# A two-part transformer kernel: row statistics of eight norms kept 128x512 instead of 128x4

## The reference

```python
def _layer_norm(x, eps):
    mu = jnp.mean(x, axis=-1, keepdims=True)
    xc = x - mu
    return xc * lax.rsqrt(jnp.mean(xc * xc, axis=-1, keepdims=True) + eps)

def _rmsnorm(x, w):
    return x * lax.rsqrt(jnp.mean(x * x, -1, keepdims=True) + NORM_EPS) * w
```

## Time and profile before

| | us |
|---|---|
| median of 3 runs | 3008.81 |
| lowest, highest | 3007.4, 3012.82 |
| the profiled execution, its own time | 3008.55 |
| its span in the profile | 3006.8 |

### The profile page before, as it was taken

One profiled execution on the slowest core, in us unless ns is written; L12 is line 12 of the kernel. 1 busy time (PEld: TensorE's weight loads), 2 busy tenths in 40 slices (PEclk: granted clock), 3 DMA queues, 4 the chain that ended last, 5 costly groups with the idle time before them and its releaser, 6 DMA issues.

```text
span 3006.8 us, 38616 instructions
## 1 busy us (share of the span) xinstructions
PE 2838.2 (94%) x16220; PEld 2225.1 (74%) x16220; DVE 1456.4 (48%) x2103; ACT 1023.1 (34%) x1526; POOL 1.4 (0%) x6
## 2 busy tenths in 40 slices
PE   5999999998999999979999999999999879899998
PEld 1476577657888877768788887888877568688886
DVE  1148444754533456454454345533455676454344
ACT  0035434543322335412432223322234432332222
POOL 0000000000000000000000000000000000000000
PEclk9999989997999999899899999999999899899998
DMA  9221112111323222100122323223232100122322
GB/s 387 85 70 64 49 56 77 64 49 50 108 85 110 79 85 96 41 32 29 64 92 88 109 80 96 98 83 110 78 95 77 57 22 4 57 91 84 109 81 70
DMA packets 65116, 245.02 MB, mean 81 GB/s; under 512 B 7216, under 2 KB 7344, under 8 KB 63536
## 3 DMA queue, kind: packets, MB, share of 16 engines
q1 hardware_dynamic: 64656, 238.36, 23.5%
q0 software_dynamic: 288, 4.19, 0.4%
HBM read 240.43 MB, written 2.10 MB: 81 GB/s over the span
## 4 chain that ended last, share of the span: by engine, by line
PE 91%; DVE 4%; ACT 3%; issue 1%; DMA 1%; SPq 0%; ACTq 0%; DVEq 0%
PE bank L367 89%; ACT work L1392 1%; DVE work L1961 1%; PE bank L550 1%; DMA work<-w_ada 1%; ACT weights_high L1426 1%; DVE residual L1961 1%; DVE weights_low L1975 0%; ACT normed L1392 0%; ACT silu_gate L1392 0%; ACT L1392 0%; PE bank L1150 0%; DVE work L2348 0%; DVE work L2650 0%; DVE silu_gate L2664 0%
## 5 line engine op out<-in xcount | busy, mean ns | idle before, releaser
L367 PE MATMUL bank<-normed,weights_high 128*128 128x512 f32 x4848 | 1544.1, 400 | 25.6 <-ACT normed L1392 22.0
L367 PEld LDWEIGHTS bank<-normed,weights_high 128*128 128x128 f32 x4848 | 914.8, 191 | 252.3 <-issue 62.3
L367 PE MATMUL bank<-normed,weights_low 128*128 128x512 f32 x2424 | 957.4, 395 | 0.0
L1975 DVE TENSOR_TENSOR weights_low<-ring,weights_high 128x1024 fp32r<-128x1024 f32 (+2 forms) x431 | 483.9, 1126 | 526.1 <-ACT weights_high L1426 522.8
L1426 ACT ACTIVATE weights_high<-ring 128x1024 fp32r<-128x1024 f32 (+2 forms) x431 | 420.7, 979 | 931.4 <-PE bank L367 931.3
L367 PEld LDWEIGHTS bank<-normed,weights_low 128*128 128x128 f32 x2424 | 463.4, 191 | 98.8
L367 PE MATMUL bank<-hidden,weights_high 128*128 128x512 f32 x1408 | 433.4, 389 | 0.0
L367 PEld LDWEIGHTS bank<-hidden,weights_high 128*128 128x128 f32 x1408 | 264.3, 188 | 54.8
L2190 DVE TENSOR_TENSOR silu_gate<-bank,rstd 128x512 f32<-128x512 f32 x176 | 120.9, 691 | 340.8 <-PE bank L367 336.0
L367 PE MATMUL bank<-hidden,weights_low 128*128 128x512 f32 x704 | 273.9, 389 | 0.0
L367 PE MATMUL bank<-work 64*64 64x64 f32 (+7 forms) x1632 | 161.2, 320 | 4.2 <-DVE work L2650 3.2
(11 more groups left out here) (222 smaller groups left out, 1897.7 us busy)
## 6 DMA issues: line engine op xcount, KB each, us to landing
ring<-w_k SPq DMA_DIRECT2D x303, 512.0 KB, 3.2
work<-w_ada SPq DMA_DIRECT2D x6, 4096.0 KB, 20.9
ring<-w_d SPq DMA_DIRECT2D x64, 384.0 KB, 3.0
ring<-w_d SPq DMA_DIRECT2D x64, 320.0 KB, 2.9
work<-dft_in POOLq DMA_DIRECT2D x2, 2048.0 KB, 8.1
constants<-cst_in SPq DMA_DIRECT2D x1, 2304.0 KB, 8.0
residual<-x_in SPq DMA_DIRECT2D x1, 2048.0 KB, 13.3
out_dram<-residual SPq DMA_DIRECT2D x8, 256.0 KB, 2.0
```

The source lines that it names most:

```text
L367: return pe.matmul(o, lhsT, rhs, start=start, stop=stop, skip_group_check=True)
L1975: ve.tensor_tensor(WL[:, u % SPLIT, 0:w], RING[:, u % SLOTS, 0:w], WH[:, u % SPLIT, 0:w].bitcast(F32), ALU.subtract).then_inc(unit_split, 1)
```

## The change

The layer norms and the feed-forward pre-norms no longer go through 128x4. Their mean square is made as the mean is, with `onesD` as the stationary tile and the 128x512 squares as the moving one: eight products in a layer norm, one on the summed squares in a feed-forward. The result is 128x512, the same in every partition. ScalarE's root and VectorE's reciprocal run over 128x512, the reciprocal straight into `RSTD[:, 1, :]`, which VectorE's products read. The spreading products of these eight norms, the wait for them, and the copy to `RSTD[:, 1, :]` in the feed-forwards go. Mixer pre-norms and post-norms stay as they are (`compact`).

```diff
+        def compact(norm):
+            return norm[0] == "post" or norm[0] == "pre" and norm[1].startswith("mix")
...
             def layer_norm(norm, after):
                 mean_over_features(norm, "mean", lambda k: X[:, k, :], PS[6], after)
-                rms_of(norm, *[(tile(k), act_done("sq", norm, k)) for k in range(KT)])
-                spread(norm)
+                mean_over_features(norm, "ms", lambda k: tile(k), PS[7], lambda k: act_done("sq", norm, k))
...
                         unit_product(u0 + j, ffn_bank("pair", q, j // 2, j % 2)[:], lambda x: H[:, x, :],
-                                     lambda x: H[:, KT + x, :], 0, KT, KT, ("pre", f) if q == 0 and j == LEAD + 1 else None)
+                                     lambda x: H[:, KT + x, :], 0, KT, KT)
                         if q == 0 and j == LEAD:
-                            rms_of(("pre", f), (tile(0), dve_done("sum", f)))
+                            pe.wait_ge(*dve_done("sum", f))
+                            step(mm(PS[7][:], cst("onesD"), tile(0)), "ms", ("pre", f))
...
             def root(norm):
                 act.wait_ge(*pe_done("ms", norm))
-                a(RSTD[:, 0, 0:4], PS[7][:, 0:4], ACT.Sqrt, "sd", norm,
+                w = TT if compact(norm) else T
+                a(RSTD[:, 0, 0:w], PS[7][:, 0:w], ACT.Sqrt, "sd", norm,
...
                         root(("pre", f))
-                        kept_rstd(("pre", f))
...
             def reciprocal_std(norm):
                 dve.wait_ge(*act_done("sd", norm))
-                d(ve.reciprocal(RSTD[:, 0, 4:8], RSTD[:, 0, 0:4]), "rstd", norm, chain=False)
+                if compact(norm):
+                    d(ve.reciprocal(RSTD[:, 0, 4:8], RSTD[:, 0, 0:4]), "rstd", norm, chain=False)
+                else:
+                    d(ve.reciprocal(RSTD[:, 1, :], RSTD[:, 0, :]))
...
                 reciprocal_std(norm)
-                dve.wait_ge(*pe_done("spread", norm))
                 for k in range(KT + 1):
                     if k < KT and first:
-                        d(stt(tile(8 + k), tile(8 + k), MOD[:, l, 8 + k:9 + k], PS[7][:], ALU.mult, ALU.mult),
+                        d(stt(tile(8 + k), tile(8 + k), MOD[:, l, 8 + k:9 + k], RSTD[:, 1, :], ALU.mult, ALU.mult),
                           "t", f"first{l}", k, chain=False)
                     elif k < KT:
-                        d(stt(X[:, k, :], tile(8 + k), v("lng", 8 * l + k), PS[7][:], ALU.mult, ALU.mult),
+                        d(stt(X[:, k, :], tile(8 + k), v("lng", 8 * l + k), RSTD[:, 1, :], ALU.mult, ALU.mult),
                           "xn", norm, k, chain=False)
...
                 low(lows_first + LEAD + SPLIT)
-                dve.wait_ge(*act_done("rstd", ("pre", name)))
+                if compact(("pre", name)):
+                    dve.wait_ge(*act_done("rstd", ("pre", name)))
```

## The result

| | before | after |
|---|---|---|
| median, us | 3009.66 | 2986.49 |
| lowest, highest | 3007.4, 3012.82 | 2984.06, 2987.57 |
| the profiled execution, its own time | 3008.55 | 2984.06 |
| its span | 3006.8 | 2982.3 |

The ratio is 0.9921, 95% interval 0.9906 to 0.9936: faster by some 23 us, where 17 had been forecast. The direction came out as forecast, and so did what each of the eight places costs after the change; some 5 us of the gain were in no step of the sum.

What follows compares the result with a forecast made beforehand. TensorE was taken to bound the kernel, busy 94% of the span. Layer norms 13.2 plus feed-forward pre-norms 3.9 gave 17.1 us, so 2991.7 us against the median, with 2986 to 2999 for 8 in 10.

Steps and rivals of the forecast that it cites:

- the sum: Whole kernel: layer norms 13.2 plus feed-forward pre-norms 3.9 give 17.1 us saved, other moved work costed at nothing.
- What bounds the kernel: TensorE, busy 94% of the span: norm latency counts in the layer norms, only TensorE time in the dense feed-forward stream.
- The layer norms, 13.2 us: Four layer norms: chains shorter by 4.45, 2.54, 1.71 and 4.46 us, together 13.2 us.
- The new path: Each layer norm, first square product to VectorE's next product: 1.28 + 14 x 0.429 + 0.80 + 3.38 = 11.47 us.
- Full clock in the wide products: Layer norms: all 16 wide instructions of a mean square run at full clock, 0.429 us apart.
- the first rival: Layer norms: the 1.4 us silence lowers the clock, wide instructions at half clock, 27.4 us more, 3019.1 us; chance 0.05.
- the partly slow one: Layer norms: a quarter of the 64 wide instructions at half rate gives back 6.9 us, 2998.6 us; chance 0.12.
- VectorE late but covered, 4 us: Feed-forwards: VectorE's later first scaling hides behind 4 us of cover at bank 0, cost nothing.
- The rule on the reciprocal: 128x512 reciprocal: the skill's repeat count of 8 gives 4.27 us, layer norms 9.5 us; the trace's 3.35 us was preferred.
- The four pre-norms, 3.9 us: Feed-forward pre-norms: 1.83 us of small stretches out, one 0.86 us wide product in, 0.97 us each, 3.9 us together.
- The restarts: Rival, dense work after the layer norms: TensorE regains full clock sooner, 13 us at most, 2978.5 us; chance 0.03.
- the forecast's own 2988 to 2995: Whole kernel: range around the forecast, as another execution of either kernel can stand 2 to 3 us apart; chance 0.76.

Runs made afterwards that it cites:

- e1: Only the four layer norms changed, against the kernel before, feed-forward pre-norms left as they were: 2996.48 us, ratio 0.9959.
- e9: Changed kernel with the reciprocal of the four feed-forward pre-norms done twice on VectorE: 2988.37 us, ratio 0.9936 against the kernel before.
- e10: Changed kernel with the reciprocal of the four feed-forward pre-norms done three times on VectorE: 3010.88 us, ratio 1.0009 against the kernel before.
- e2: Only the four feed-forward pre-norms changed, against the kernel before, layer norms left as they were: 2999.92 us, ratio 0.9967.
- e3: The changed kernel measured a second time against the kernel before, five executions: 2987.57 us, ratio 0.9926.
- e7: Changed kernel with six idle wide products behind the mean square in each layer norm: 2986.56 us, ratio 0.9923 against the kernel before.
- e8: Changed kernel with the layer norms' root and reciprocal replaced by ScalarE's exp(-ln(x + eps) / 2): 2979.92 us, ratio 0.9902 against the kernel before.
- e11: Changed kernel with the exp/ln root and three idle wide products behind each layer norm's mean square: 2976.29 us, ratio 0.9896 against the kernel before.
- e4: The kernel before measured against itself, nothing changed: 3008.25 us, ratio 0.9998.
- e5: Changed kernel with idle TensorE products, about 0.97 us each, in feed-forwards 01 and 10: 2992.16 us, ratio 0.9943 against the kernel before.
- e6: Kernel before with 1.7 us of idle TensorE products in the second half of feed-forward 10: 3006.55 against 3009.73 us, ratio 0.9991.

## Why the prediction was off

**What bounds the kernel: right.** The layer norms' latency and TensorE's time in the dense stream are where the change works directly.

**The layer norms, 13.2 us: the mechanism right, the size in part luck.** 13.4 by the medians of e1. The new path is 0.2 us shorter than worked out: 7.17 instead of 7.29 us from the first product to the root, and 0.72 instead of the 0.80 of the query norm from root to reciprocal. The old path was read from one trace, in which the clock fell unusually early in two of the four norms. Against it the gain is 13.9 us, against the other traces with the one-column form 8.1 to 10.5, and how much of e1's 13.4 lies in the norms in a typical execution is not known.

**Full clock in the wide products: right,** and the first rival (half clock, slower) and the partly slow one are refuted by PEclk 1.00 over the whole stretch in all four norms. It was the one-column form that brought the clock down, in 16 stretches of 16. The silence of 1.4 us, which lies ahead of both forms, did not do it.

**VectorE late but covered, 4 us: right.** One more reciprocal of 3.4 us is hidden, two more are not (e9, e10), and from the wait of 2.1 us the cover is 4.6. The price beyond the cover was set too low in the prediction: "at most the 3.35 us per feed-forward" left out that a wait takes the clock with it.

**The rule on the reciprocal.** The row's 3.35 us held in all four layer norms. The estimate of 4.27 us from the repeat count that the Trainium skill states (VectorE: DVE Perf Modes, First, the fixed hardware budget) would have made their gain too small by 3.7 us; by that rule, the trace disagrees.

**The four pre-norms, 3.9 us: the step that failed.** The cost was right for the place, 0.87 us in and some 1.8 out. What failed is the assumption in the sum that stretches which the change doesn't touch keep their length, so that all else stands at nothing. The second mixer alternates between full and half clock, and what it gets depends on how long the clock has been full when it starts. Taking 1 us out of feed-forwards ahead of it shifts that: 4.4 us less in the mixer, in all seven traces with the new pre-norms in which TensorE neither does idle work nor waits in the feed-forwards (after, e2, e3, e7, e8, e9, e11), with or without the layer norms, and in none of the three with the old ones (before, e1, e4). It does not come through anything in the pre-norms themselves, since idle work moves it too, in either kernel (e5, e6). By the medians e2 gained 9.9 us where the sum had 3.9; of the 6 us that are missing, the 4.4 are these, and the last 1.6 are not pinned down. The text took such shifts for noise between executions ("another execution of either kernel can stand 2 to 3 us apart") and put them into the range on both sides; here it is a fixed part of the result. The measured 2986.49 us lie below the forecast's own 2988 to 2995.

**The restarts.** That they warm sooner was set at 3 in 100, with 13 us at most. All four still start at half clock, and that the silence causes this is shown by e7. A small part of the rival is true all the same. The first feed-forward, behind the fourth of them, from the sum of squares to the post-norm, takes 363.3 us after against 365.7 and 365.2 in the two traces before, 0.9 to 1.4 us more than its 0.97 explain.

**What stays open.** Which arrival gives which course of the second mixer is read from 13 traces, not mapped, and what sets e5 and e6 (170.0 us) apart from the kernel after at nearly the same arrival is not known. Whether e7's loss in the mixers is fixed or of that one execution was not separated. Nor is it known what e6 gained beyond its idle work.

## What to carry to other kernels

Wide products with a constant stationary tile beat many one-column ones for a mean square, because they keep TensorE's clock up and leave the result where it is read; the 3.4 us of a 128x512 reciprocal is then the next thing to shorten. The gain has to be worked out from more than one trace of the kernel before: the one-column stretches alone differed by 5.9 us between two. Where a kernel has stretches that run partly at half clock, a change of 1 us ahead of them can move them by several: compare the same pair of instructions in both traces, piece by piece, before the difference is put down to the changed lines, and test with idle work of the same length.

## What was not expected of the hardware

- Idle work made a kernel no slower: 1.7 us of products into an unread bank, 3006.55 against 3009.73 us (e6).
- The length of a stretch at alternating clock comes in steps. The same 152 VectorE instructions of the second mixer took 172.5, 171.9, 170.0 or 167.6 us in 13 traces, with at most 0.22 us between those of one step, and three of the four steps go with how long the clock had been full at the start.
- A wait of 2.1 us in a dense stream cost 4.0 us in the first feed-forward, since the clock fell to 0.72 in the 5 us behind it (e10), while the 1.44 us ahead of the mean square cost no clock at all.
